# Gate and up products of the last token block as seven block products instead of eight

## What is computed

```
h2 = rmsnorm(x, norm2_g)
x = x + (silu(h2 @ w_ffn_gate) * (h2 @ w_ffn_up)) @ w_ffn_down
y = rmsnorm(x, final_norm_g)
```

## Time and profile before

| | |
|---|---|
| median of 3 runs | 3147.77 us (3146.66 to 3147.89) |
| the profiled execution | 3147.71 us, of which 3145.9 us is the span from the first to the last instruction |
| busy share of the span: PE, PE weight load, DVE, ACT, POOL | 99%, 84%, 53%, 33%, 7% |
| HBM traffic | 532.28 MB, 169 GB/s over the span |
| TensorE's granted clock | 0.998 of 2.4 GHz |
| last block's products | from about 2729.6 us to 3133 us |

### The profile page before, as it was taken

The page is one execution under the profiler, slowest core; times in us unless marked ns, Lnnn a source line. Parts: engine busy times, 40 slices in busy tenths (PEclk is TensorE's granted clock), DMA queues, the critical chain, the costliest instruction groups (busy, mean ns, idle before and its releaser), DMA issues.

```text
span 3145.9 us, 65881 instructions
## 1 busy us (share of the span) xinstructions
PE 3102.5 (99%) x27801; PEld 2640.2 (84%) x27801; DVE 1675.3 (53%) x2856; ACT 1035.2 (33%) x1893; POOL 223.9 (7%) x205
## 2 busy tenths in 40 slices
PE   8999999999999999999999999999999999999998
PEld 6777778888887888888888889998888889999997
DVE  6577554577777673355564275305666535532224
ACT  5545433444444443232231043303333313300001
POOL 0112100011111000011110000001111100000000
PEclk9999999999999999999999999999999999999999
DMA  4555443376666853554444673265444455455556
GB/s 162 168 191 171 157 157 99 103 248 212 211 217 216 265 185 95 179 168 146 146 142 158 193 251 96 93 217 179 133 130 130 140 161 179 153 189 177 177 177 196
DMA packets 272404, 532.28 MB, mean 169 GB/s; under 512 B 36208, under 2 KB 39664, under 8 KB 272112
## 3 DMA queue, kind: packets, MB, share of 16 engines
q1 hardware_dynamic: 272112, 528.07, 51.8%
HBM read 415.97 MB, written 112.08 MB: 168 GB/s over the span
## 4 chain that ended last, share of the span: by engine, by line
PE 93%; DVE 3%; ACT 2%; DMA 1%; issue 1%; SPq 0%; POOL 0%; DVEq 0%; ACTq 0%
PE PS L869 81%; PE PS L913 6%; PE PS L972 1%; PE PS L1038 1%; PE PS L1022 1%; PE PS L1212 1%; PE PS L962 1%; PE PS L1008 0%; PE PS L1219 0%; DMA wl<-weight_lo 0%; ACT L1237 0%; DVE wl L1677 0%; DMA raw<-w 0%; PE PS L906 0%; PE PS L998 0%
## 5 line engine op out<-in xcount | busy, mean ns | idle before, releaser
L869 PE MATMUL PS<-hh,wh 128*128 128x512 f32 x1864 | 749.5, 402 | 0.1
L869 PE MATMUL PS<-hh,wl 128*128 128x512 f32 x1864 | 727.5, 390 | 0.0
L869 PE MATMUL PS<-hl,wh 128*128 128x512 f32 x1864 | 727.2, 390 | 0.0
L1256 ACT ACTIVATE wh<-raw 128x512 fp32r<-128x512 f32 x452 | 283.4, 630 | 429.3 <-PE PS L869 354.1
L869 PEld LDWEIGHTS PS<-hh,wh 128*128 128x128 f32 x1864 | 349.9, 188 | 79.8 <-issue 2.1
L869 PEld LDWEIGHTS PS<-hh,wl 128*128 128x128 f32 x1864 | 350.0, 188 | 75.7
L1677 DVE TENSOR_TENSOR wl<-raw,wh 128x512 fp32r<-128x512 f32 x452 | 321.8, 714 | 164.3 <-ACT wh L1256 160.8
L869 PEld LDWEIGHTS PS<-hl,wh 128*128 128x128 f32 x1864 | 350.5, 188 | 67.8 <-issue 0.7
L869 PE MATMUL PS<-hh_last,wh 128*128 128x272 f32 x1280 | 266.0, 289 | 0.1
L869 PE MATMUL PS<-hl_last,wh 128*128 128x272 f32 x1280 | 264.6, 288 | 0.0
L869 PE MATMUL PS<-hh_last,wl 128*128 128x272 f32 x1280 | 263.1, 287 | 0.0
(11 more groups left out here) (306 smaller groups left out, 4667.3 us busy)
## 6 DMA issues: line engine op xcount, KB each, us to landing
wh<-weight_hi SPq DMA_DIRECT2D x500, 256.0 KB, 2.7
wl<-weight_lo SPq DMA_DIRECT2D x500, 256.0 KB, 3.0
raw<-w SPq DMA_DIRECT2D x178, 512.0 KB, 3.6
weight_hi<-wh SPq DMA_DIRECT2D x164, 256.0 KB, 4.3
weight_lo<-wl SPq DMA_DIRECT2D x164, 256.0 KB, 4.7
raw<-w SPq DMA_DIRECT2D x92, 256.0 KB, 3.1
gate_scratch<-gst SPq DMA_DIRECT2D x48, 256.0 KB, 3.7
gb<-gate_scratch SPq DMA_DIRECT2D x48, 256.0 KB, 4.4
```

The lines of the kernel that those rows point to most:

```text
L869: mm = pe.matmul(PS[:, bank(t) + f, 0:t.cols], wt[:, cols], mov[:, m, (t.half + f) * t.cols:(t.half + f + 1) * t.cols], start=(first and a ...
L1256: act.activation(wh[h % 4][:], src, ACT.Copy).then_inc(hi_done, 1)
```

## The change

For the last block and j = 2 to 21 the pair gate and up is no longer 16 quanta of six matmuls. It is taken as a product of two by two blocks (Winograd's form of Strassen's scheme). The weight blocks are g1, g2 (gate, planes 0 to 3 and 4 to 7) and u1, u2 (up); the activation blocks are the two halves of planes 0 to 3 (x1, x2) and of planes 4 to 7 (z1, z2), 272 tokens each. Sums of weight blocks, made anew for each j: S0 = u1+u2, S1 = S0-g1, S2 = g2-S1, S3 = g1-u1. Sums of activation blocks, made once: T0 = x2-x1, T1 = z2-T0, T2 = z2-x2, T3 = z1-T1. The seven products are P0 = g1 x1, P1 = g2 z1, P2 = S0 T0, P3 = S1 T1, P4 = S2 z2, P5 = S3 T2, P6 = u2 T3; gate is P0+P1 and P0+P3+P2+P4, up is P0+P3+P5+P6 and P0+P3+P5+P2. Each product is 4 quanta of three 272-column matmuls.

Where the work goes, for each j:
- SP loads the raw gate and up weights (2 DMAs of 512 KB, `halves_raw`), and kept pairs only for P0, P1 and P6.
- POOL makes the four 128x512 sums (`weight_sums`) and four multiplications by `nrs` of 128x272 (`scaled_sevens`).
- ACT rounds the four sums to `sh` (`sums_rounded`), copies P0 and P2 out of PSUM, and does the tanh and `fh` as before.
- DVE takes the rests `sl` of the sums (`sums_rest`), five adds that read PSUM and two that don't (`seven`), and the three wide operations `e1`, `acc` and `fl` (`sevens_done`).

Once, around the start of the block, DVE makes the T sums of each plane (24 operations of 128x272, `halves`), ACT rounds them and POOL takes the rests (16 each). PSUM banks of the seven are fixed by OWN_BANK. `kept_again` keeps its ring of four, now counted over the loaded pieces alone. `seven` is emitted for two j at a time; down of the first group now follows the first two j of the second. The new generators run last in the merged lists of their engines. Left out of the diff below: semaphores, buffer placement, the counting of the ring, `halves` and `halves_rest`.

```diff
+OWN_BANK = {"P0": 0, "P1": 3, "P2": 2, "P3": 1, "P4": 2, "P5": 0, "P6": 1}
+FIRST7 = GROUPS[0]
...
+            if t.spread == 3:
+                before, bank = t, OWN_BANK[t.stage]
+                self.banks[t.n] = bank
+                self.held[t.n] = [holder[bank].n]
+                holder[bank] = t
+                continue
...
+    def seven(self, b, s, j):
+
+        pairs = (j, j + 1)
+        for jj in pairs:
+            for m in range(7):
+                t = self.tile(f"P{m}", b, jj)
+                t.h, t.spread = 1, 3
+        products = [(jj, m) for jj in pairs for m in range(7)]
+        for at in range(0, 14, 2):
...
+            for i, (jj, m) in enumerate(products[at:at + 2]):
+                h = 2 * (len(self.units) - 1) + i
+                first = group_unit(s) + 2 * (jj - sum(GROUPS[:s]))
+                if m in MADE:
+                    self.made[h] = jj, MADE[m]
+                else:
+                    key = ((first + (m == 6), KD, 0),)
+                    self.where[h] = self.kept[key], int(m > 0)
...
+                if b == NB - 1 and s:
+                    if j % 2 == 0:
+                        self.seven(b, s, sum(GROUPS[:s]) + j)
+                    if s == 1 and j == 0:
+                        self.down(b, 0)
+                    continue
...
+        def made_tag(h):
+            j, u = plan.made[h]
+            last = made_before(h)
+            ready = plan.first_of(j) - 20.0 + 6.0 * u if last is None else plan.piece[last][-1] + 1.3
+            return max(ready, sum_tag(j, u) + 4.0)
+
+        def sum_tag(j, u):
+            at = (0, 2, 3, 1)[u]
+            return plan.first_of(j) - 26.0 + 4.0 * at if j == FIRST7 else plan.first_of(j - 1) + (3.4, 6.6, 12.4, 15.8)[at]
+
+        def after(j, at):
+            q0 = plan.first_of(j)
+            return q0 + (at if at < 28 or q0 + 28 in plan.product else 28 + (at - 28) / 2)
+
...
+            def halves_raw():
+                for j in range(FIRST7, NFF):
+                    for i in (1, 0):
+                        if j == FIRST7:
+                            yield Q["late", 0] + 3.0 - i
+                            if i:
+                                sp.wait_ge(lo_done, 2 * len(plan.fresh))
+                        else:
+                            yield plan.first_of(j - 2 if j > FIRST7 + 1 else j - 1) + (21.0, 11.5)[i] - (0 if j > FIRST7 + 1 else 28)
+                            sp.wait_ge(s_f, 4 * (j - FIRST7) - (0, 2)[i])
+                        u = group_unit(group_of(j)) + 2 * (j - sum(GROUPS[:group_of(j)])) + i
+                        sp.dma_start(raw[i][:], w[u]).then_inc(s_ld[i], 16)
+
...
+                hi, lo = (sh[MADE[m]], sl[MADE[m]]) if m in MADE else (wh[plan.ring[piece]], wl[plan.ring[piece]])
+                if m in (0, 1, 4):
+                    b = NB - 1
+                    mv, at, c0 = (hh[b], hl[b]), k + (0, 4, 4)[(0, 1, 4).index(m)], HT * (m == 4)
+                else:
+                    i = {2: 0, 3: 1, 5: 2, 6: 3}[m]
+                    mv, at, c0 = (tph[i], tpl[i]), k, 0
+                cols = slice(128 * (p % 4), 128 * (p % 4) + 128)
+                for a, (wt, mov) in enumerate(((hi, mv[0]), (hi, mv[1]), (lo, mv[0]))):
+                    mm = pe.matmul(PS[:, bank(t), 0:HT], wt[:, cols], mov[:, at, c0:c0 + HT],
+                                   start=(first and a == 0), stop=(n == t.last and a == 2))
...
+            def sevens():
+                for j in range(FIRST7, NFF):
+                    q0, i, done = plan.first_of(j), j - FIRST7, (NB - 1) * NFF + j
+                    for what, after, out in (("P0", 4, p0), ("P2", 12, p2)):
+                        t = tile(what, NB - 1, j)
+                        yield q0 + after + 0.05
+                        act.wait_ge(dense, q0 + after)
+                        if i and what == "P0":
+                            act.wait_ge(*freed(tile("P3", NB - 1, j - 1)))
+                        elif i:
+                            act.wait_ge(p_v, 2 * i)
+                        act.activation(out[:], psv(t), ACT.Copy).then_inc(evac["A"], 1)
+                    yield q0 + 23.8
+                    act.wait_ge(p_r, 4 * i + 2)
+                    if i == 0:
+                        act.wait_ge(f_v, FIRST7)
+                    tanh_table()
+                    act.activation(e2[:, 0:MT], e1[:, 0:MT], ACT.Tanh, scale=0.5).then_inc(f_t, 1)
+
+            def sevens_done():
+                for j in range(FIRST7, NFF):
+                    yield after(j, 33.4)
+                    act.wait_ge(f_acc, (NB - 1) * NFF + j + 1)
+                    act.activation(fh[NB - 1][:, act_plane(j), 0:MT], acc[:, 0:MT], ACT.Copy).then_inc(f_hi, 1)
+                log_table()
+
+            def sums_rounded():
+                for h, (j, u) in plan.made.items():
+                    last = made_before(h)
+                    yield made_tag(h)
+                    if last is None:
+                        act.wait_ge(t_lo, 16)
+                        act.wait_ge(n1_rs, 2 * len(USES))
+                    else:
+                        act.wait_ge(dense, plan.piece[last][-1] + 1)
+                    act.wait_ge(s_f, made_sum(j, u))
+                    act.activation(sh[u][:], sf[u][:], ACT.Copy).then_inc(s_hi, 1)
...
+            def weight_sums():
+                a11, a12, a21 = raw[0][:, 0:WP], raw[0][:, WP:WU], raw[1][:, 0:WP]
+                for j in range(FIRST7, NFF):
+                    n = 4 * (j - FIRST7)
+                    for u in (0, 3, 1, 2):
+                        yield sum_tag(j, u)
+                        if u == 0:
+                            pool.wait_ge(s_ld[1], 16 * (j - FIRST7 + 1))
+                        if u == 3:
+                            pool.wait_ge(s_ld[0], 16 * (j - FIRST7 + 1))
+                        if j > FIRST7:
+                            pool.wait_ge(s_lo, n - 3 + u)
+                        if u == 0:
+                            pool.tensor_tensor(sf[0][:], a21, raw[1][:, WP:WU], ALU.add).then_inc(s_f, 1)
+                        if u == 3:
+                            pool.tensor_tensor(sf[3][:], a11, a21, ALU.subtract).then_inc(s_f, 1)
+                        if u == 1:
+                            pool.wait_ge(s_f, n + 1)
+                            pool.tensor_tensor(sf[1][:], sf[0][:], a11, ALU.subtract).then_inc(s_f, 1)
+                        if u == 2:
+                            pool.wait_ge(s_f, n + 3)
+                            pool.tensor_tensor(sf[2][:], a12, sf[1][:], ALU.subtract).then_inc(s_f, 1)
+
+            def scaled_sevens():
+                for j in range(FIRST7, NFF):
+                    for what, out, cols, at in (("P1", e1, slice(0, HT), 10.2), ("P4", e1, slice(HT, MT), 21.5),
+                                                (None, up, slice(HT, MT), 26.6), ("P6", up, slice(0, HT), 29.4)):
+                        yield after(j, at)
+                        if what:
+                            pool.wait_ge(*freed(tile(what, NB - 1, j)))
+                        else:
+                            pool.wait_ge(p_v, 2 * (j - FIRST7) + 2)
+                        pool.tensor_tensor(out[:, cols], out[:, cols], nrs[:, cols], ALU.mult).then_inc(p_r, 1)
...
+            def seven(j):
+                q0, i = plan.first_of(j), j - FIRST7
+                p1, p3, p4, p5, p6 = (tile(f"P{m}", NB - 1, j) for m in (1, 3, 4, 5, 6))
+                yield q0 + 8.1
+                dve.wait_ge(dense, q0 + 8)
+                dve.wait_ge(*freed(tile("P0", NB - 1, j)))
+                dve.wait_ge(f_acc, (NB - 1) * NFF + j)
+                dve.tensor_tensor(e1[:, 0:HT], p0[:], psv(p1), ALU.add).then_inc(evac["V"], 1)
+                yield q0 + 16.1
+                dve.wait_ge(dense, q0 + 16)
+                dve.tensor_tensor(u2[:], p0[:], psv(p3), ALU.add).then_inc(evac["V"], 1)
+                yield q0 + 17.3
+                dve.wait_ge(*freed(p3))
+                dve.wait_ge(*freed(tile("P2", NB - 1, j)))
+                dve.tensor_tensor(e1[:, HT:MT], u2[:], p2[:], ALU.add).then_inc(p_v, 1)
+                yield q0 + 20.1
+                dve.wait_ge(dense, q0 + 20)
+                dve.wait_ge(p_v, 2 * i + 1)
+                dve.tensor_tensor(e1[:, HT:MT], e1[:, HT:MT], psv(p4), ALU.add).then_inc(evac["V"], 1)
+                yield q0 + 24.1
+                dve.wait_ge(dense, q0 + 24)
+                dve.tensor_tensor(u3[:], u2[:], psv(p5), ALU.add).then_inc(evac["V"], 1)
+                yield q0 + 25.3
+                dve.wait_ge(*freed(p5))
+                dve.tensor_tensor(up[:, HT:MT], u3[:], p2[:], ALU.add).then_inc(p_v, 1)
+                yield q0 + 28.1
+                dve.wait_ge(dense, q0 + 28)
+                dve.tensor_tensor(up[:, 0:HT], u3[:], psv(p6), ALU.add).then_inc(evac["V"], 1)
+
+            def sevens_done():
+                for j in range(FIRST7, NFF):
+                    i, n = j - FIRST7, (NB - 1) * NFF + j
```

(69 more changed lines are left out.)

116 lines of the change are left out of this document (97 added, 19 removed).

## The result

The changed kernel takes 3184.86 us (median of 4, 3184.34 to 3186.08), the kernel before in the same job 3147.41 us (3146.66 to 3147.89): a ratio of 1.012 [1.0102, 1.0137], **slower by 37.5 us**. The forecast was 3175 us, slower by 27, in a range from 3141 to 3198. The profiled executions, 3186.08 and 3147.71 us, are 38.4 us apart.

The account below looks back on a forecast made before the run. PE, busy 99% of the span, was taken to bound the kernel: 3147.7 - 30 for removed matmuls + 57 for PE's waits on POOL and DVE turns gave 3175 us, range 3141 to 3198.

Parts of the forecast that it names:

- Removed work, -30.0: Last block's seven products: 240 matmuls fewer at 0.125 us each, -30.0 us.
- DMA, 0: Weight loads of each j: 249 GB/s needed, most seen 267 to 273, so no loss; +17 us at only 230.
- Turns, 11.7 us per j: POOL and two-SBUF-input DVE operations pass one at a time, overlapping 0.14 us: 11.7 us per j against PE's 10.5.
- The walk of the queues, +57: Fixed orders of POOL, DVE and ACT stepped through: PE waits 12.0 us in a group of four, +57 us in all.
- T sums, 0: Sums of activation blocks around the block's start, hidden while DVE stands mostly idle: 0, at most 5 us.
- Clock still 1.00: Sign in the last block: PE's window shows idle time for the first time, with the granted clock unchanged at 1.00.
- 20 x 1.2: Turns packed without a gap, beyond PE's time over the 20 j: takes back 23 of the 30 us.
- a group with its down: PE time of four j and their down product: 4 x 10.5 + 24.1 = 66.3 us, before 72.3.
- the turns fall into slack: Rival: sums made a j ahead, so only the very last group end waits; 3119 us, chance 0.10.

Follow-up runs that it names:

- e1: Changed kernel, all nine DVE operations of a j with two SBUF inputs reading one from an idle PSUM bank (output not the reference's); 3128.82 us.
- e3: Changed kernel with POOL's four multiplications by `nrs` left out (output not the reference's); 3126.74 us.
- e4: Changed kernel with the rests of the weight sums later in DVE's order, behind the adds that free PSUM; 3167.05 us.
- e9: Changed kernel with one added wait: POOL's S0 waits until DVE has written `acc` of the j but one before; 3176.78 us.
- e10: Changed kernel with both the added wait of S0 for `acc` and the later rests of the weight sums; 3164.30 us.
- experiment 5: Three edits of the T sums' place in the changed kernel, at the start of the block: e5 3191.72, e8 3184.61, e11 3183.90 us.
- e11: As e8, with SP's stores of block 2's output rows 24 quanta later in its queue; 3183.90 us.
- e2: Changed kernel with only the four rests of the weight sums reading PSUM in place of a second SBUF input (output not the reference's); 3158.79 us.
- e5: Changed kernel with all T sums tagged later and closer together in DVE's order; 3191.72 us.
- e8: Changed kernel with only the third and fourth T sums later, behind block 2's last residual adds, each a little denser; 3184.61 us.

## Why the prediction was right, and where it was off

- **Removed work, -30.0**: 240 matmuls fewer, pace 0.125 us in the P products too (2900.65, 2900.78, 2900.90 are successive starts). Right.
- **DMA, 0**: right to 2 us: between 2704 us and the end the waits for `wl` make 3.6 us, before 1.5. The reason given was too narrow. 273 GB/s isn't the most that the trace of before shows: its window from 2754 to 2758 us has 390 GB/s at share 1.04 (a transfer counts where it starts, so a short window can pass 1), with PE busy all the time. After, the window above has 410. So there was more room than the prediction took, and for those microseconds more than its 358 GB/s.
- **Turns, 11.7 us per j**: right in kind and in size (0.14 to 0.16 us of overlap; e1 takes them away and comes out at 3128.82). Held for the whole instruction, as the Trainium skill (SBUF — State Buffer, "Who interferes with whom") has it, `acc` would have ended 0.73 us after POOL's sum; the trace gives 0.59. But 11.7 isn't all of it: e3, e4, e9 and e10 show that the order of the turns decides over 8 (e9) to 18 us (e4) of the loss.
- **The walk of the queues, +57**: it gave each place, and the third and fourth j 13.6 us apart (13.68). P0's wait 2.4 (2.32; the fourth's 1.38 in two of four groups), P4's 0.5 (0.33), down's 1.4 and 3.7 (1.46, 3.34). By the tally waits cost +53.5, of which 3.4 are at the start of the block, so the walk's places gave about 50: the term was some 7 us too large. It fails further off: without the scalings it was 15 us out, since it left POOL ahead of `acc`.
- **T sums, 0**: this step failed. They cost 3.26 us of wait, and in this execution the block starts at low clock behind it (46 matmuls in the 8 us from 2734.33, at 0.79, where the kernel before does 59), 2.5 us by the tally. The prediction's bound of 5 is about what they cost, though no placing of them won it back (experiment 5). DVE "stands mostly idle" there hid the point: it is busy for 22.6 of the 50 us from 2704 to 2754 before, with block 2's residual adds among them, and PE waits for such an add behind the T sums.
- **"Clock still 1.00"**: this step failed, and it is what was missing from the sum: +12.9 us, all of it in the block, where the clock before was 1.00 throughout. Behind each wait of 3.3 to 3.4 us of this kernel the clock was granted at 1.2 GHz for some microseconds (0.50 at 2911 to 2914), behind those of 2.3 us in some places.
- **Small slips**: 20 x 1.2 is 24, not 23, and a group with its down is 42 + 24.1 = 66.1 us (before 72.1). The forecast rests on neither.

So the sum for waits and work, 27 us, was 23.5, the clock added 12.9 and the rest 1.5. Right in sign and in mechanism, and low by 10.5 us: waits put 3.5 too high, and a term of 13 that wasn't in the sum. That the two partly cancel is luck.

As for the rivals: "the turns fall into slack" foresaw 3119, and e1 and e3 (3128.82, 3126.74) show it is what happens once the turns are out of the way or fewer. The turns are what kept it from happening.

## What to carry to other kernels

Where VectorE and GpSimd both read two operands from SBUF, count their time as one queue and compare it with TensorE's: here 11.7 against 10.5 us lost 56 us (18 of them by the order alone), and 9.2 against 10.5 kept 21 of 24. Then see who goes first: a wait that holds back the operation nobody waits for can be a gain (8 us), and one operand from PSUM takes an operation out of the queue altogether. And price waits of TensorE like these at more than their length, since the clock may fall behind them, unless another such wait follows that takes the loss up.

## What the runs showed of the hardware

- A wait of PE is often followed by a low clock. In the kernel after, the five waits of 3.3 to 3.4 us (four in down products, one at the start) were each followed by 8 us at a mean clock of 0.63 to 0.82. Of seven waits of 2.2 to 2.3 us five were followed by 1.00 and two by 0.79; in e11 all six waits of 2.2 to 2.5 us by 0.79 or 0.80. Behind those of 1.4 to 1.6 us ahead of a product it stayed at 0.95 to 1.00. One fall costs 1.4 to 2.8 us in the tally.
- The length of the wait alone doesn't decide it: the waits of 3.28 us in e2 and 3.27 in e3 at the start of the block, and one of 3.36 us in e5 (2836.85), were followed by 8 us at 1.00, and two of four waits of 1.87 us in e4 by 0.79.
- What a fall costs in time depends on what bounds the stretch. From the third P0 of a group to the fourth it is 13.67 to 13.71 us in all eight cases of the kernel after and e11, though the clock fell in six of them. From the wait for `fl` to the next group's third P0 it is 44.6 to 44.9 us where the 8 us behind that wait had a mean clock of 0.79 to 0.82, and 45.8 to 46.1 where they had 0.61 to 0.65. So a gain in waits can come out much smaller: e11 has 8 us less of them than e8 and is 0.7 us faster.
- The shared access goes to whoever comes first, by a hair: S0, right behind POOL's last scaling, went ahead of `acc`, which waits for that same scaling, in 18 of 20 j (1.71 to 1.75 us for `acc`), the other two being the last, for which no S0 follows. With one added hop for S0 it was never ahead (725 ns in e9).
